# Products of a two-way recurrence, interleaved over all four 64x64 quadrants of TensorE

## The reference

```python
def wkv_scan(state0, r, decay, kk, b, v, k, reverse):
    def step(S, inp):
        r_t, w_t, kk_t, b_t, v_t, k_t = inp
        sa = jnp.einsum("bhvk,bhk->bhv", S, kk_t)
        S = (S * w_t[:, :, None, :] - sa[..., None] * b_t[:, :, None, :]
             + v_t[..., None] * k_t[:, :, None, :])
        return S, jnp.einsum("bhvk,bhk->bhv", S, r_t)
...
y_sum = y if y_sum is None else y_sum + y
```

## Time and profile before

| | us |
|---|---|
| median of 3 executions | 1715.99 (1715.91 to 1730.39) |
| the profiled execution | 1721.18 |
| its span | 1719.4 |
| PE busy | 1604.4 |
| DVE busy | 916.6 |
| recurrence, turns -2 to 11 | 275.3 to 594.1 |
| mean granted clock of TensorE | 0.937 of full speed |

### The profile page before, as it was taken

One profiled execution on the slowest core, in us unless ns is written; L12 is line 12 of the kernel. 1 busy time (PEld: TensorE's weight loads), 2 busy tenths in 40 slices (PEclk: granted clock), 3 DMA queues, 4 the chain that ended last, 5 costly groups with the idle time before them and its releaser, 6 DMA issues.

```text
span 1719.4 us, 36464 instructions
## 1 busy us (share of the span) xinstructions
PE 1604.4 (93%) x15540; PEld 1355.4 (79%) x15540; DVE 916.6 (53%) x1465; ACT 541.7 (32%) x890; POOL 208.4 (12%) x206
## 2 busy tenths in 40 slices
PE   7899998999999969999998999999958999999997
PEld 4787976999999857778877888778747788888886
DVE  1624214565667545788887223676443455556222
ACT  3422233212121223444433223545543322223221
POOL 0000002223233001111111111000001111111011
PEclk8899997878999988999999998999969999999998
DMA  8232101212110112222222222222001222222221
GB/s 328 74 142 74 61 14 51 101 52 101 53 53 4 52 50 74 74 98 89 84 96 92 95 90 90 79 76 74 25 25 51 97 98 94 91 93 89 101 101 66
DMA packets 33885, 139.73 MB, mean 81 GB/s; under 512 B 2272, under 2 KB 2784, under 8 KB 33248
## 3 DMA queue, kind: packets, MB, share of 16 engines
q1 hardware_dynamic: 33616, 135.76, 22.3%
q10 hardware_dynamic: 144, 2.10, 0.3%
HBM read 135.75 MB, written 2.10 MB: 80 GB/s over the span
## 4 chain that ended last, share of the span: by engine, by line
PE 81%; DVE 11%; ACT 4%; issue 3%; DMA 0%; POOL 0%; DVEq 0%; ACTq 0%; SPq 0%
PE bank L621 53%; PE bank L754 12%; DVE ffn_sb L2433 4%; PE bank L631 2%; DVE w_up L2039 1%; PE bank L941 1%; ACT w_up L1370 1%; PE bank L584 1%; PE bank L1255 1%; PE bank L860 1%; PE bank L882 1%; PE bank L1244 1%; PE bank L862 1%; PE bank L566 1%; PE bank L884 1%
## 5 line engine op out<-in xcount | busy, mean ns | idle before, releaser
L621 PE MATMUL bank<-hf_hi,w_up 128*128 128x512 f32 x1376 | 426.2, 391 | 0.0
L621 PEld LDWEIGHTS bank<-hf_hi,w_up 128*128 128x128 f32 x1376 | 259.9, 189 | 53.7
L621 PE MATMUL bank<-hf_lo,w_up 128*128 128x512 f32 x688 | 271.8, 395 | 5.5 <-DVE w_up L2039 4.7
L621 PE MATMUL bank<-act_hi,w_down 128*128 128x512 f32 x704 | 218.5, 392 | 0.0
L754 PE MATMUL bank<-arena 64*64 64x32 f32 (+2 forms) x4992 | 195.4, 239 | 18.1 <-POOL arena L1882 6.9
L754 PEld LDWEIGHTS bank<-arena 64*64 64x64 f32 x4992 | 189.2, 151 | 22.4 <-issue 14.6
L2039 DVE TENSOR_TENSOR w_up<-ring,w_up 128x1024 fp32r<-128x1024 f32 x88 | 108.1, 1229 | 105.8 <-ACT w_up L1370 105.7
L1370 ACT ACTIVATE w_up<-ring 128x1024 fp32r<-128x1024 f32 x88 | 93.0, 1058 | 217.4 <-PE bank L621 217.4
L621 PEld LDWEIGHTS bank<-hf_lo,w_up 128*128 128x128 f32 x688 | 130.0, 189 | 39.6 <-DVE w_up L2039 13.3
L621 PEld LDWEIGHTS bank<-act_hi,w_down 128*128 128x128 f32 x704 | 133.4, 189 | 27.9
L2433 DVE SCALAR_TENSOR_TENSOR ffn_sb<-ffn_sb 128x512 f32<-128x512 f32 x176 | 151.5, 861 | 6.3 <-ACT ffn_sb L1611 0.8
(11 more groups left out here) (318 smaller groups left out, 2373.4 us busy)
## 6 DMA issues: line engine op xcount, KB each, us to landing
ring<-w SPq DMA_DIRECT2D x92, 1024.0 KB, 4.7
ring<-w SPq DMA_DIRECT2D x32, 704.0 KB, 4.0
arena<-w SPq DMA_DIRECT2D x2, 3072.0 KB, 22.4
x<-xT SPq DMA_DIRECT2D x1, 2048.0 KB, 11.6
arena<-w SPq DMA_DIRECT2D x2, 1024.0 KB, 19.2
x<-xT ACTq DMA_DIRECT2D x1, 2048.0 KB, 9.0
outT<-x SPq DMA_DIRECT2D x4, 512.0 KB, 2.7
arena<-ctxT SPq DMA_DIRECT2D x1, 1024.0 KB, 7.2
```

The costliest lines, as they stand in the source:

```text
L621: ins = mm(out, w[:, a, k, :], of_block(b, k0 + k), start=first and k == 0 and m == 0, stop=last and k == n - 1 and m == 2)
```

## The change

The products of a head that come from the state, the update or bh stay in their quadrant ("straight"). Those with kh, kr or the values go from rows of one half to columns of the other ("crossing"), for which the values' transposes are written crosswise at the beginning (`values_turned`). The two kinds of opposite directions are issued in turn: for each pair j, two straight products of one direction and two crossing ones of the other. So `state_in`, `state_terms`, `turned` and `scores` have two parts, 0 and 1, each with both directions, and the second part finishes what the first has begun; `results` has a third, straight part. Part 0 waits for both directions, part 1 for a semaphore of part 0.

```diff
+        CROSSED = ((HALVES[0], HALVES[1]), (HALVES[1], HALVES[0]))
...
+            def state_in(n, part):
+
+                if part == 0:
+                    for d in both:
+                        done("kr", d, n + 1)
+                        done("S", d, n)
+                else:
+                    pe.wait_ge(s["state_half"], 2 * n + 2)
+                straight, across = part, 1 - part
+                sc, other = scans[straight], scans[across]
+                v_in = v_tok[:, place(across, n) // L]
                 for j in range(NJ):
...
                     for r in HALVES:
...
+                        a = mm(bank[straight][3][r, at], sc.ktrt[r, n % 3, j, 0:L], sc.S[r, n % 2, j, :],
+                               start=part == 0 and j == 0, stop=part == 1 and j == NJ - 1)
+                    for r, o in CROSSED:
+                        b = mm(bank[across][3][o, at], other.kr[r, n % 2, j, 0:L], v_in[r, j, :],
+                               start=part == 0 and j == 0, stop=part == 1 and j == NJ - 1)
+                a.then_inc(s[f"gu_mm{straight}" if part else "state_half"], 1)
+                b.then_inc(s[f"gu_mm{across}" if part else "state_half"], 1)
...
+                        a = mm(bank[straight][0][r, at], sc.bh[r, j, :], sc.ktrt[r, q % 3, j, 0:n], start=True, stop=True)
+                    for r, o in CROSSED:
+                        b = mm(bank[across][1][o, at], other.kh[r, j, :], other.ktrt[r, q % 3, j, 0:n], start=True,
+                               stop=True)
+                a.then_inc(s[f"nr_mm{straight}"], 1)
+                b.then_inc(s[f"kr_mm{across}"], 1)
```

`state_terms`, `turned` and the first two parts of `results` have the same form. The order of PE's loop:

```diff
                 if n >= 0:
-                    for d in both:
-                        state_in(n, d)
+                    state_in(n, 0)
                 if inv:
                     for d in both:
                         nx(m, d, 2)
                 if n >= 0:
-                    for d in both:
-                        updates(n, d)
+                    state_in(n, 1)
                 if inv:
                     for d in both:
                         dx(m, d, 2)
                 if ada:
                     ada_parts(n)
+                if n >= 0:
+                    for d in both:
+                        updates(n, d)
+                if 0 <= m < NC - 1:
+                    turned(m, 0)
                 if 0 <= n < NC - 1:
-                    for d in both:
-                        state_terms(n, d)
+                    state_terms(n, 0)
                 if 0 <= m < NC - 1:
-                    for d in both:
-                        turned(m, d)
+                    turned(m, 1)
+                if 0 <= n < NC - 1:
+                    state_terms(n, 1)
...
                 if n >= NCC:
-                    for d in both:
-                        results(n, d)
+                    results(n, 0)
                 if inv:
                     for d in both:
                         nx(m, d, 4)
+                if n >= NCC:
+                    results(n, 1)
+                if inv:
                     for d in both:
                         dx(m, d, 4)
+                if n >= NCC:
+                    results(n, 2)
...
                 if prep:
-                    for d in both:
-                        scores_b(q, d)
+                    scores(q, 0)
...
                 if prep:
-                    scores_k(q, 0)
+                    scores(q, 1)
...
-                if prep:
-                    scores_k(q, 1)
```

On DVE the second addition of results goes from before to behind level 4, and the masked scores take another place:

```diff
                 if prep and q >= NCC:
-                    for d in both:
-                        scores_out(q, d, 0)
+                    scores_out(q, 0, 0)
...
+                if prep and q >= NCC:
+                    scores_out(q, 1, 0)
...
+                    scores_out(q, 1, 1)
                     scores_out(q, 0, 1)
                 if inv:
                     for d in both:
                         y_last(m, d)
-                if prep:
-                    scores_out(q, 1, 1)
```

More of the change, by code:

```diff
@@ L754, in tiles, with crossed_tiles @@
                         last = mm(out(j, r), lhs(j, r), rhs(j, r), start=True, stop=True)
+                return last
+            def crossed_tiles(out, lhs, rhs):
+                for j in range(NJ):
+                    for r, o in CROSSED:
+                        last = mm(out(j, o), lhs(j, r), rhs(j, r), start=True, stop=True)
                 return last
@@ L871, in updates, with state_terms @@
                       lambda j, r: sc.gu[r, j, :]).then_inc(s[f"gu_mm{d}"], 1)
-            def state_terms(n, d):
-                sc = scans[d]
-                done("gu", d, 2 * n + 2)
-                done("tok", d, n + 1)
-                v_in = v_tok[:, place(d, n) // L]
+            def state_terms(n, part):
+                if part == 0:
+                    for d in both:
+                        done("gu", d, 2 * n + 2)
+                        done("tok", d, n + 1)
+                else:
+                    pe.wait_ge(s["terms_half"], 2 * n + 2)
+                straight, across = part, 1 - part
+                sc, other = scans[straight], scans[across]
+                v_in = v_tok[:, place(across, n) // L]
@@ new lines, in state_terms @@
+                        a = mm(bank[straight][3][r, at], sc.tok[r, 0, j, :], sc.gu[r, j, :],
+                               start=part == 0 and j == 0, stop=part == 1 and j == NJ - 1)
+                    for r, o in CROSSED:
+                        b = mm(bank[across][3][o, at], other.tok[r, 1, j, :], v_in[r, j, :],
+                               start=part == 0 and j == 0, stop=part == 1 and j == NJ - 1)
+                a.then_inc(s[f"ds_mm{straight}" if part else "terms_half"], 1)
+                b.then_inc(s[f"ds_mm{across}" if part else "terms_half"], 1)
@@ new lines, in results @@
+            def results(n, part):
+                at_half = 4 * (n - NCC) + 2 * part
+                if part == 0:
+                    for d in both:
+                        done("gu", d, 2 * n + 2)
+                        done("nr", d, min(n + 2, NC))
+                        pe.wait_ge(s[("ada_row", "mod")[d]], (8, 1)[d] + min(n + 2, 8))
+                else:
+                    pe.wait_ge(s["results_half"], at_half)
+                if part == 2:
+                    for d, sc in enumerate(scans):
+                        for j in range(NJ):
+                            for r in HALVES:
+                                last = mm(bank[d][0][r, L * j:L * j + L], sc.gu[r, j, :],
+                                          sc.nr[r, n % 2, j, L:2 * L], start=False, stop=j == NJ - 1)
+                        last.then_inc(s[f"y_mm{d}"], 1)
+                    return
+                straight, across = part, 1 - part
+                sc, other = scans[straight], scans[across]
+                v_in = v_tok[:, place(across, n) // L]
+                for j in range(NJ):
+                    at = slice(L * j, L * j + L)
+                    for r in HALVES:
+                        a = mm(bank[straight][0][r, at], sc.S[r, n % 2, j, :], sc.ktrt[r, n % 3, j, L:2 * L],
+                               start=part == 0 and j == 0, stop=False)
+                    for r, o in CROSSED:
+                        b = mm(bank[across][0][o, at], v_in[r, j, :], other.kr[r, n % 2, j, L:2 * L],
+                               start=part == 0 and j == 0, stop=False)
+                a.then_inc(s["results_half"], 1)
+                b.then_inc(s["results_half"], 1)
@@ L2277, in _ @@
                         x_turned(m, d, 4)
+                if n >= NCC + NCX // 2:
+                    for d in both:
+                        second_result(n, d)
+                if inv:
                     for d in both:
```

99 lines of the change are left out of this document (42 added, 57 removed).

## The result

Median 1748.1 us (4 executions, 1743.8 to 1754.3) against 1717.7 for the kernel before on the same chip (4 executions): ratio 1.017, 95% interval 1.014 to 1.021. The prediction was 1693, range 1679 to 1718: the wrong sign, and 30 us above the range. The profiled execution took 1747.2 us (before 1721.2).

What follows compares the result with a forecast made beforehand. PE, busy 93% of the span, was taken as the bound, with DVE close behind in the recurrence. Savings over the turns summed to 22.3 us, plus 0.7 net: 23 off the median 1716.0 gave 1693.0, range 1679 to 1718.

Steps and rivals of the forecast that it cites:

- The pace: Woven products on four quadrants: 15.2 ns a record instead of 29.2, and 27.2 instead of 54.4 for 128 columns.
- The sum at the full clock: Turn 7's stretches at clock 1.00 (23.1 us before), added up part by part: about -0.9 us.
- (A): Level 2 to 3 of turn 7: 6.7 us against 6.53, second mask follows sooner, so nothing gained.
- (B): Level 3 to 4 of turn 7: DVE makes the keys, results already lay under that, so 0.
- (C): Level 4 to 5 of turn 7: two parts of the results now stand between the levels' products, a price of +0.9 us.
- (D): Scores between the level 5 products in turn 7: 0.87 us instead of 1.74, and 0.2 less waiting: -1.1 us.
- rival 3: DVE is the bound sooner than thought, POOL's work stretching the score outputs, so score and tail gains halve: 1706 us; 15%.
- (E): Turn 7's tail (second scores half, level 6, state products): 5.75 us until the next level 2 product, -0.65.
- The clock: Recurrence's mean granted clock 0.89; PE saves twice as much at the lower level, so 5 us of gain.
- Rival 2: PE waits more, so turns 4 to 9 all fall to clock 0.81; 24 us eats the gain: 1717 us; 17%.
- Instruction issue at twice the pace: A cost in the recurrence set against the clock's gain, together with more PE waits; +0.7 us net of these.
- Rival 1: Quadrants don't overlap, or dispatch sets the pace; the reordering by itself costs +35 us: 1751 us; 10%.

Runs made afterwards that it cites:

- the filled kernel: Kernel after plus products of zero use in PE's waits (ahead of level 3's second products, under the keys, before level 6's second products); 1733.7 us, ratio 1.010.

## Why the prediction was wrong, step by step

- **The pace** (15.2 and 27.2 ns): right, 14.5 and 27.4. What followed for time was wrong, as the pace is not what bounds a turn.
- **The sum at the full clock**: near. Put together from turns 7 to 9 of the kernel after and of the one with the clock held, where these had the full clock, the stretches of a turn 7 are 7.35, 4.18, 3.28, 4.30 and 3.40, together 22.5 against 23.06: -0.55 where I had -0.9.
  - (A) +0.2 by my working, booked as 0 (its terms up to the end of the copy add up to 3.88, not 3.97, a slip of 0.1); measured +0.8 (7.35 and 9.37 with the ada product, against 6.53 and 8.54). My 5.7 for the state's start was good (5.9 in turn 8 of the filled kernel), but its four operations take 2.2 us instead of 1.7: the first one with both operands in SBUF (L2287 above) takes 0.81 and the second 0.50, both beside products of POOL, where before, with POOL idle, they took 0.42 each.
  - (B) 0; measured -1.0. The keys take 2.5 us instead of 3.2. POOL works beside them for 2.2 of the 2.5 us, before for all of them; whether that is the reason was not tested.
  - (C) +0.9; measured +0.9 (3.28).
  - (D) -1.1; measured -0.1 (4.30 for 4.42). This step was wrong in kind. The masked score of direction 1 was put between level 5's transposes and level 6's mask, where DVE now works without a break from 565.24 on. So in this stretch DVE is the bound, as rival 3 feared, through the new place of the score and not through slower operations; (D) and (E) together gave 1.3 us of the 1.75.

```profile
565.24 0.69 DVE L2278 TENSOR_TENSOR arena<-bank,k_ 128x512 f32<-128x512 f32 x1 [0.61 <-PE bank L850]
565.85 0.59 DVE L2242 TENSOR_TENSOR arena<-bank,arena 128x128 f32<-128x128 f32 x2
566.36 0.76 DVE L2249 STREAM_TRANSPOSE arena<-arena 128x256 f32<-128x256 f32 x2
567.05 0.69 DVE L2278 TENSOR_TENSOR arena<-bank,k_ 128x512 f32<-128x512 f32 x1
567.66 0.72 DVE L2264 COPY_PREDICATED arena<-k_,arena 128x128 f32<-128x128 uint32 x2
568.17 0.58 DVE L2235 TENSOR_TENSOR arena<-bank,k_ 128x128 f32<-128x128 f32 x2
```

  - (E) -0.65; measured -1.2.
- **The clock**: the step that failed. The sum left the granted clock at 0.89 and booked it as a gain of 5 us (products at the lower level save twice), less 2 for more waits and something for the issue, "+0.7 net". But the waits that the change makes for PE, and the halts, took the clock itself to 0.72 over the recurrence. Rival 2 had the mechanism and about the right price (2.9 us a turn for 0.11, 26 for 1.00; turn 7: 28.4 instead of 22.5 at 0.74, 23 for 1.00), but not the extent: I let six turns fall to 0.81, and all fell, turns 10 and 11 to 0.63 (+10.7 us alone). Against it I had set turn 10, "waits of PE as well": those were 0.5 us in 18.4, under a third of one wait of 1.58.
- **Instruction issue at twice the pace** was named, inside that +0.7. Measured, the halts grew by 6 us in the kernel after (14.1 for 7.9), by 9 with the old order, and by 21 where idle products were added (29.3). Beside the long ones the clock fell as well.
- **Rival 1's order alone**: +35 predicted, +35 measured, but by luck. In turn 7 it is +2.7 for my +3.7: (A) +2.2 for 2.3, (C) +1.3 for 1.9, the tail -1.2 for -0.4, (B) -1.0 and (D) +1.4, which I hadn't. The rest came from halts (13.7 for 7.9) and a lower clock (0.87 for 0.89). The linear scale between the two paces, turning at 21 ns, was wrong: at 14.5 ns the time was 30 us longer, not 23 shorter.
- **The signs**: "turn 7 longer than 23.1" and "clock under 0.85" were the two that came.

What stays open: why the clock falls in some turns of a kernel and not in others with the same waits (turn 9 of the kernel after kept it from level 2 to 3, turn 8 did not; with straight pairs turn 7 kept it behind waits of 1.14 and 0.77 us). And how the loss divides: cutting the transfers took 7 us of halts and 9 us of the recurrence from the kernel after at nearly the same clock, but no run changed the clock alone. The 7 us that the untouched rest was shorter go with its clock: behind the recurrence the kernel before took longest of all sixteen, 1125.2 us at 0.95, and the one with straight pairs was shortest, 1112.2 at 0.97; why that clock differs isn't known.

## What to carry to other kernels

A faster product pays only where PE is what ends the stretch; elsewhere it becomes a wait, and such waits can cost the clock of what stands behind them: here waits of 0.6 to 1.7 us, a few in each turn, took it from 0.89 to 0.72. So before making PE's groups shorter, list for each who ends it, and count the new idle time as a price at the low clock, not as slack. When a clock is in doubt, cut the turn at a fixed operation of another engine and compare the stretches one by one: at one clock they repeat from turn to turn (8.53 or 8.54 us from level 2 to 3 in six turns of before), so a longer one shows where the clock or a halt has struck.

## What the runs showed of the hardware

- Four 64x64 tiles of float32, two straight and two crossing, run at 14.5 ns a record for 64 columns and 27.4 for 128, twice the pace of two (29.2 and 54.4). A crossing tile shares rows with one neighbour and columns with the other, and neither slowed it here.
- Idle products took 15 us off the recurrence of one kernel (352 to 337) and nothing off that of another (319 and 320).
- PE halted for up to 3.6 us in the kernel after, and 4.2 with idle products, for want of instructions beside transfers of 1 MB; PE went on 1.2 to 1.6 us after a packet of 16,384 bytes had landed. The Trainium skill, "Runtime: NRT & Kernel Launch", section "Instruction fetch mechanics", has blocks of 16 KiB fetched ahead at a cost that is "mostly hidden". The trace shows such packets (q8, 0.02 MB), but halts of 7.9 us in sum before and 14.1 after, of 1.0 and 6.8 where the transfers were cut: nearly hidden only at the old pace with the DMA engines free.
- DVE's operation on the state with both operands in SBUF took 0.42 us alone, and 0.81 and 0.50 beside products of POOL.
- In the recurrence of the kernel before the granted clock fell 7 times, in that of the kernel after 17 times, all but once during or shortly behind a wait of PE of 0.5 to 3.6 us, whether for a semaphore or for instructions. Not every such wait had a fall behind it.
